# A hybrid decoder layer on one core: the MLP output of seven blocks as seven quarter products of sums

## The chip, the cores and the metric

One NeuronCore of one Trainium2 chip runs the whole layer in one launch. The metric is the device time of that launch in microseconds (us). Engines are named as the profile names them: PE is TensorE, DVE is VectorE, ACT is ScalarE, POOL is GpSimd, SP is SyncE, which here only issues transfers.

## The reference, cut to what matters

The layer works on 512 tokens of 1024 features: a gated linear recurrence and a sparse attention side by side, an output projection, and then the MLP, which is the part that the change touches.

```python
hm = rms_norm(x, mlp_norm_g[l])                                     # 512 x 1024
x = x + jnp.square(jax.nn.relu(hm @ w_mlp_in[l])) @ w_mlp_out[l]    # 1024 x 4096, 4096 x 1024
return rms_norm(x, final_norm_g)
```

## The kernel before

All weights come from HBM as one stream of slabs, 128 partitions x 1024 float32 (512 KB), in the order of use. Slab n goes into `raw[n % 4]`. ScalarE copies it to float32r (`hi`, L553, the high part `whi`), VectorE subtracts that from it (`lo`, L792, the rest, `wlo`), and TensorE multiplies in three passes (`three`, L1154 to L1156): high by high, high by low, low by high. Activations are split in the same way. So every product costs three matmuls, and every slab one ScalarE and one VectorE instruction of 128x1024.

Ahead of the MLP come 55 slabs (`PLAN`) with the mixers as side work. The last of them are those of `w_o`; their results are added to the residual `y` by VectorE (L884). Then TensorE transposes `y`, ScalarE and VectorE split it to `hTh` and `hTl`, and the MLP begins.

The MLP runs over eight blocks of 512 hidden features (`block_` on each engine, seven times in a loop and once more behind it). A block has eight slabs:

- m = 0 to 3, the hidden product: each slab gives 128 hidden features for all 512 tokens, 8 x 3 = 24 matmuls of 512 columns into bank m. ScalarE takes the relu into `rt` (L773), VectorE squares it into `hv` (L1118), ScalarE copies that to float32r `hh` (L775), VectorE subtracts for `hl` (L1121).
- m = 4 to 7, the output product: slab 4 and 5 hold the block's first and second 256 hidden features for output columns 0 to 511, slab 6 and 7 for columns 512 to 1023. Four token tiles x two feature tiles x three passes are 24 matmuls each. Banks 4 to 7 take the first half of the columns, banks 0 to 3 the second. After slab 5 and slab 7 VectorE adds four banks to `y`, scaled by each token's norm factor `r2y` (L1135), eight instructions a block.

Slabs are split three ahead (`AHEAD`) of the one that TensorE works on. Each engine works off its own instructions in the order in which they are written; semaphores count what is done: `raw_in` (slab landed), `hi_done`, `lo_done`, `full[b]` (a bank's sum is complete), `free[b]` (a bank was read out). SP asks for slab n when slab n - 4 has been split (L440). Behind the last block ScalarE sums the squares of `y`, GpSimd forms the norm factor, VectorE scales (L1107), and SP writes `out`.

Of the kernel before, what the change touches and what calls it, by code (L numbers as in the profile page):

```python
# [18 lines left out]
F32 = mybir.dt.float32  # L19
F32R = mybir.dt.float32r  # L20
# [5 lines left out]
P = 128  # L26
T = 512
# [39 lines left out]
V_COLS = 32  # L67
WIN = 2 * P
# [4 lines left out]
def build(nc, x, slabs, vecs, consts, onehot, rel_bias, final_g, out):  # L73
    with ExitStack() as ctx:
# [6 lines left out]
        def sem(name):  # L81
# [61 lines left out]
        hv = [place(f"hv{i}", 189 + 2 * i, T) for i in range(2)]  # L143
# [30 lines left out]
        raw_in = [sem(f"raw_in{s}") for s in range(SLOTS)]  # L174
        hi_done, lo_done, slab_used = sem("hi_done"), sem("lo_done"), sem("slab_used")
# [11 lines left out]
                 "rik_done ry_done rf_done pool_step iqh_done aqh_done kdh_done ikh_done ikl_done")  # L187
# [154 lines left out]
        def used_up(n, it=None):  # L342

            if it is not None:
                m = n - NPLAN
                if m in (4, 6):
                    return slab_used, it * 2 + (BY_COUNT + m // 2 - 1)
                if m == 5:
                    return full[7], it + (MB2[3] + 1)
                if m in (-1, 7):  # L350
                    return full[3], it * 2 + (MB if m == -1 else MB + 2)
                return full[m], it * 2 + (MB + 1)
            if n in by_count:
                return slab_used, by_count[n]
            b, u = c1_bank if tiles[n] == "side" else tiles[n][-1]
            return full[b], u + 1

        def loop_blocks(eng, body):

            with eng.Fori(0, NFB - 1, 1) as it:  # L360
                body(it, False)
            body(NFB - 1, True)
# [32 lines left out]
        mxl3 = mxl[:, :].rearrange("p (k t) -> p k t", k=KD_)  # L395
        hh3 = hh[:, :].rearrange("p (k t) -> p k t", k=4)
# [31 lines left out]
        def _(sp):  # L428
# [5 lines left out]
            def load(n, dyn=None):  # L434

                s = n % SLOTS
                if n >= SLOTS:

                    sp.wait_ge(lo_done, n - SLOTS + 1 if dyn is None else dyn * PER_FB + (n - SLOTS + 1))
                sp.dma_start(raw[s][:, :], slabs[n] if dyn is None else  # L440
                             slabs[bass.ds(dyn * PER_FB + n, 1), :, :].rearrange("a p c -> (a p) c")
                             ).then_inc(raw_in[s], 16)
# [14 lines left out]
            with sp.Fori(0, NFB, 1) as it:  # L457
                for m in range(PER_FB):
                    load(NPLAN + m, it)
# [8 lines left out]
        def _(pool):  # L468
# [61 lines left out]
            for n in range(NPLAN):  # L530
                for s in side[n]:
                    do_side(s)
            pool.wait_ge(S["sq_done"], SQ_Y + NT)
# [11 lines left out]
        def _(act):  # L545
            def hi(n, it=None):

                s = n % SLOTS
                arrived = 16 * (n // SLOTS + 1)
                act.wait_ge(raw_in[s], arrived if it is None else it * (16 * PER_FB // SLOTS) + arrived)  # L550
                if n >= SLOTS:
                    act.wait_ge(*used_up(n - SLOTS, it))
                act.copy(whi[s][:, :], raw[s][:, :]).then_inc(hi_done, 1)  # L553
# [213 lines left out]
            def block_(it, last):  # L767
                for m in range(PER_FB):
                    if not (last and m + AHEAD >= PER_FB):
                        hi(NPLAN + m + AHEAD, it)  # L770
                    if m < 4:
                        act.wait_ge(full[m], it * 2 + (MB + 1))
                        act.activation(rt[m % 2][:, :], bank[m][:, :], ACT.Relu).then_inc(free[m], 1)  # L773
                        act.wait_ge(S["hv_done"], it * 4 + (m + 1))
                        act.activation(hh3[:, m, :], hv[m % 2][:, :], ACT.Copy).then_inc(S["hh_done"], 1)  # L775

            loop_blocks(act, block_)
            for t in range(NT):
                act.wait_ge(free[4 + t], MB2[t] + NFB)
                square(y3[:, t, 0:512], 512, ssf[:, t:t + 1])  # L780
            for t in range(NT):
                act.wait_ge(free[t], MB + 2 * NFB)
                square(y3[:, t, 512:D], 512, ssg[:, t:t + 1])
# [3 lines left out]
        def _(dve):  # L787
            def lo(n, it=None):

                s = n % SLOTS  # L790
                dve.wait_ge(hi_done, n + 1 if it is None else it * PER_FB + (n + 1))
# [318 lines left out]
            def block_(it, last):  # L1110
                for m in range(PER_FB):
                    if not (last and m + AHEAD >= PER_FB):
                        lo(NPLAN + m + AHEAD, it)
                    if m < 4:
                        dve.wait_ge(free[m], it * 2 + (MB + 1))
                        if m:
                            dve.wait_ge(S["hl_done"], it * 4 + m)
                        dve.tensor_tensor(hv[m % 2][:, :], rt[m % 2][:, :], rt[m % 2][:, :],  # L1118
                                          ALU.mult).then_inc(S["hv_done"], 1)
                        dve.wait_ge(S["hh_done"], it * 4 + (m + 1))  # L1120
                        dve.tensor_tensor(hl3[:, m, :], hv[m % 2][:, :], hh3[:, m, :].bitcast(F32),  # L1121
                                          ALU.subtract).then_inc(S["hl_done"], 1)
                    if m in (5, 7):
                        half = (m - 5) // 2
                        if half == 0:
                            dve.wait_ge(S["hl_done"], it * 4 + 4)
                        for t in range(NT):
                            if half == 0:
                                b = 4 + t
                                dve.wait_ge(full[b], it + (MB2[t] + 1))  # L1130
                            else:
                                b = t
                                dve.wait_ge(full[b], it * 2 + (MB + 2))
                            yy = y3[:, t, half * 512:(half + 1) * 512]
                            dve.scalar_tensor_tensor(out=yy, in0=bank[b][:, :], scalar=r2y[:, t:t + 1], in1=yy,  # L1135
                                                     op0=ALU.mult, op1=ALU.add).then_inc(free[b], 1)
                            if last and half == 1 and t:
                                final(t - 1)

            dve.wait_ge(S["ry_done"], 1)  # L1140
            dve.wait_ge(fg_in, 16)
            loop_blocks(dve, block_)
# [4 lines left out]
        def _(pe):  # L1147
# [251 lines left out]
            def block_(it, last):  # L1399
                for m in range(PER_FB):  # L1400
                    n = NPLAN + m
                    s = n % SLOTS
                    pe.wait_ge(lo_done, it * PER_FB + (n + 1))
                    if m < 4:
                        wh, wl = slab_view(whi, s, KD_), slab_view(wlo, s, KD_)
                        pe.wait_ge(free[m], it * 2 + MB)
                        for q, k in enumerate(MLP_K):
                            if m == 0:
                                pe.wait_ge(free[k], mlp_bank[k][1] + 1)
                            ins = three(bank[m][:, :], wh[:, k, :], wl[:, k, :], hTh3[:, k, :], hTl3[:, k, :],  # L1410
                                        q == 0, q == KD_ - 1)
                        ins.then_inc(full[m], 1)
                    else:
                        wh, wl = slab_view(whi, s, 2), slab_view(wlo, s, 2)
                        first, k0 = m % 2 == 0, 2 * (m % 2)
                        for t in range(NT):
                            for kk in range(2):
                                k = k0 + kk
                                if m < 6 and t == 0:
                                    pe.wait_ge(S["hl_done"], it * 4 + (k + 1))  # L1420
                                b = 4 + t if m < 6 else t
                                if first and kk == 0:
                                    pe.wait_ge(free[b], it + MB2[t] if m < 6 else it * 2 + (MB + 1))
                                ins = three(bank[b][:, :], hh3[:, k, t * P:(t + 1) * P], hl3[:, k, t * P:(t + 1) * P],
                                            wh[:, kk, :], wl[:, kk, :], first and kk == 0, k == 3)
                                if k == 3:
                                    ins.then_inc(full[b], 1)
                        if first:
                            ins.then_inc(slab_used, 1)

            loop_blocks(pe, block_)
# [84 lines left out]
```

## Time and profile before

| | |
|---|---|
| device time, median of 3 runs | 795.92 us (795.9 to 798.9) |
| the profiled execution | 796.67 us, its span 794.6 us |
| PE busy | 760.7 us, 96% |
| VectorE busy | 468.0 us, 59% |
| ScalarE busy | 302.2 us, 38% |
| GpSimd busy | 57.3 us, 7% |

The span is the time from the first to the last recorded instruction; the device time has some 2 us around it. Busy time of PE is the union of records that overlap each other, since matmuls are pipelined; the cost of one is read from the distance between the starts of two neighbours. "Idle before" in the grouped rows is the time that the engine stood still in front of such an instruction, and behind the arrow is what ended it.

### The profile page before, as it was taken

What the parts mean: (1) busy time and instruction counts of PE and PEld (TensorE: products, weight loads), DVE (VectorE), ACT (ScalarE), POOL (GpSimd) and SP (SyncE); (2) the same over time, 40 slices, a digit from 0 to 9 for tenths busy, and PEclk for the clock granted to TensorE, in tenths of its full rate; (3) what the DMA queues carried; (4) which work ended last, traced back from release to release, by engine and by line L of the source; (5) the groups of instructions that cost most, each with busy time, mean ns of one, the idle gap of its engine ahead of it and who ended that gap; (6) DMA issues with size and microseconds to landing.
All of it is one profiled execution on the core that took longest, in us unless ns stands there. A gap on an engine that the chain in (4) does not pass through costs nothing.

```text
span 794.6 us, 9959 instructions
## 1 busy us (share of the span) xinstructions
PE 760.7 (96%) x3686; PEld 636.5 (80%) x3686; DVE 468.0 (59%) x756; ACT 302.2 (38%) x495; POOL 57.3 (7%) x94
## 2 busy tenths in 40 slices
PE   5999999899997999999999999999999999999995
PEld 5788888887776788888888888888888888888884
DVE  4567878649999885334834545545445454445444
ACT  6453334547433344433312722323231423232231
POOL 3000010011001144400000000000000000000003
PEclk9999999999997999999999999999999999999998
DMA  7422111212122121112542232333233232323202
GB/s 276 160 80 81 54 54 53 80 54 91 43 85 75 54 80 54 54 59 75 168 178 80 77 109 79 106 100 106 85 97 105 89 106 79 106 89 103 72 1 106
DMA packets 20720, 71.46 MB, mean 90 GB/s; under 512 B 2344, under 2 KB 3536, under 8 KB 20688
## 3 DMA queue, kind: packets, MB, share of 16 engines
q1 hardware_dynamic: 19120, 67.88, 25.7%
q10 hardware_dynamic: 1568, 3.15, 1.1%
q8 instruction: 20, 0.33, 0.2%
q14 instruction: 12, 0.10, 0.0%
HBM read 68.91 MB, written 2.11 MB: 89 GB/s over the span
## 4 chain that ended last, share of the span: by engine, by line
PE 83%; DVE 11%; issue 2%; ACT 2%; DMA 0%; POOL 0%; DVEq 0%; POOLq 0%; ACTq 0%; SPq 0%
PE bank L1154 24%; PE bank L1156 24%; PE bank L1155 24%; PE bank L1283 3%; PE bank L1371 2%; DVE sc L948 2%; DVE small L945 2%; PE bank L1162 1%; DVE wlo L792 1%; DVE sc L935 1%; PE bank L1169 1%; PE bank L1355 1%; DVE aqs L842 1%; PE bank L1356 1%; DVE hO L1049 1%
## 5 line engine op out<-in xcount | busy, mean ns | idle before, releaser
L792 DVE TENSOR_TENSOR wlo<-raw,whi 128x1024 fp32r<-128x1024 f32 x119 | 146.2, 1229 | 112.2 <-ACT whi L553 106.7
L1154 PE MATMUL bank<-hTh,whi 128*128 128x512 f32 (+1 forms) x456 | 181.0, 397 | 3.1 <-DVE aqs L842 1.9
L1156 PE MATMUL bank<-hTh,wlo 128*128 128x512 f32 (+1 forms) x456 | 178.7, 392 | 0.0
L1155 PE MATMUL bank<-hTl,whi 128*128 128x512 f32 (+1 forms) x456 | 178.5, 391 | 0.0
L553 ACT CAST whi<-raw 128x1024 fp32r<-128x1024 f32 x119 | 124.2, 1044 | 139.3 <-PE bank L1156 139.1
L1154 PEld LDWEIGHTS bank<-hTh,whi 128*128 128x128 f32 (+1 forms) x456 | 86.0, 189 | 23.1 <-issue 4.4
L1156 PEld LDWEIGHTS bank<-hTh,wlo 128*128 128x128 f32 (+1 forms) x456 | 85.8, 188 | 18.7
L1155 PEld LDWEIGHTS bank<-hTl,whi 128*128 128x128 f32 (+1 forms) x456 | 86.0, 188 | 18.4 <-issue 0.5
L1154 PE MATMUL bank<-whi,hh 128*128 128x512 f32 x256 | 99.6, 389 | 0.0
L1155 PE MATMUL bank<-wlo,hh 128*128 128x512 f32 x256 | 99.6, 389 | 0.0
L1156 PE MATMUL bank<-whi,hl 128*128 128x512 f32 x256 | 99.6, 389 | 0.0
L1118 DVE TENSOR_TENSOR hv<-rt 128x512 f32<-128x512 f32 x32 | 22.1, 692 | 67.6 <-ACT rt L773 67.6
L1135 DVE SCALAR_TENSOR_TENSOR y<-bank,small,y 128x512 f32<-128x512 f32 x64 | 46.7, 747 | 25.9 <-PE bank L1156 25.9
L1155 PEld LDWEIGHTS bank<-wlo,hh 128*128 128x128 f32 x256 | 48.1, 188 | 10.0
L1154 PEld LDWEIGHTS bank<-whi,hh 128*128 128x128 f32 x256 | 48.1, 188 | 9.9
L1156 PEld LDWEIGHTS bank<-whi,hl 128*128 128x128 f32 x256 | 48.1, 188 | 9.9
L773 ACT ACTIVATE rt<-bank 128x512 f32<-128x512 f32 x32 | 19.1, 597 | 86.4 <-PE bank L1156 86.4
L1154 PE MATMUL bank<-whi,hTh 128*128 128x512 f32 x96 | 38.1, 397 | 2.0 <-DVE iqs L842 2.0
L1156 PE MATMUL bank<-whi,hTl 128*128 128x512 f32 x96 | 37.5, 391 | 0.0
L1155 PE MATMUL bank<-wlo,hTh 128*128 128x512 f32 x96 | 37.4, 390 | 0.0
L729 ACT ACTIVATE et<-bank 128x128 f32<-128x128 f32 (+3 forms) x32 | 14.0, 436 | 60.0 <-PE bank L1162 59.7
L1121 DVE TENSOR_TENSOR hl<-hv,hh 128x512 fp32r<-128x512 f32 x32 | 22.2, 693 | 22.4 <-ACT hh L775 22.4
(182 smaller groups left out, 1030.8 us busy)
## 6 DMA issues: line engine op xcount, KB each, us to landing
raw<-slabs SPq DMA_DIRECT2D x119, 512.0 KB, 3.3
xs<-x SPq DMA_DIRECT2D x4, 512.0 KB, 4.9
y<-x ACTq DMA_DIRECT2D x1, 2048.0 KB, 8.9
out<-ys SPq DMA_DIRECT2D x3, 512.0 KB, 2.6
bt<-bias_rows ACTq DMA_DIRECT2D x1, 1024.0 KB, 5.2
cst<-consts SPq DMA_DIRECT2D x1, 608.0 KB, 9.6
fg<-final_g SPq DMA_DIRECT2D x1, 512.0 KB, 7.3
out<-ys SPq DMA_DIRECT2D x2, 256.0 KB, 2.1
```

Source lines behind the costliest of these rows:

```text
L553: act.copy(whi[s][:, :], raw[s][:, :]).then_inc(hi_done, 1)
L773: act.activation(rt[m % 2][:, :], bank[m][:, :], ACT.Relu).then_inc(free[m], 1)
L792: dve.tensor_tensor(wlo[s][:, :], raw[s][:, :], whi[s][:, :].bitcast(F32), ALU.subtract).then_inc(lo_done, 1)
L945: dve.max(mx8[:, 8 * (i - 1):8 * i], sc_of(i)).then_inc(S["max_done"], 1)
L948: dve.match_replace(sc_of(i), mx8[:, 8 * (i - 1):8 * i], sc_of(i), TAKEN).then_inc(S["rep_done"], 1)
L1118: dve.tensor_tensor(hv[m % 2][:, :], rt[m % 2][:, :], rt[m % 2][:, :], ALU.mult).then_inc(S["hv_done"], 1)
L1121: dve.tensor_tensor(hl3[:, m, :], hv[m % 2][:, :], hh3[:, m, :].bitcast(F32), ALU.subtract).then_inc(S["hl_done"], 1)
L1135: dve.scalar_tensor_tensor(out=yy, in0=bank[b][:, :], scalar=r2y[:, t:t + 1], in1=yy, op0=ALU.mult, op1=ALU.add).then_inc(free[b], 1)
L1154: pe.matmul(dst, lh, rh, start=start, stop=False)
L1155: pe.matmul(dst, lh, rl, start=False, stop=False)
L1156: return pe.matmul(dst, ll, rh, start=False, stop=stop)
L1283: ins = pe.matmul(bank[bu[0]][:, 64 * v:64 * v + 64].rearrange("p (n h) -> p n h", h=H), un, rhs, start=True, stop=True)
```

## The change

In the first seven blocks the output product is cut into quarters. The block's squared activations A (512 tokens x 512 features) are four quarters A00, A01, A10, A11 of 256 x 256 (first index: half of the tokens, second: half of the features), the weights B (512 features x 1024 columns) four slabs B11, B12, B21, B22. Instead of eight quarter products there are seven of sums, in this order (`PRODUCTS` names them 1, 7, 4, 5, 6, 3, 2):

| order | left side | right side | banks |
|---|---|---|---|
| 1 | A00 | B11 | 0, 1 |
| 2 | A00 - A10 (`sa`) | B22 - B12 (in `br12`) | 4, 5, kept over all blocks |
| 3 | A11 | `wt4` = `wt2` - B21 | 2, 3 |
| 4 | A10 + A11 (`sb`) | `wt1` = B12 - B11 | 0, 1 |
| 5 | `sb` - A00 (`sx`) | `wt2` = B22 - `wt1` | 2, 3 |
| 6 | A01 - `sx` (`sa` again) | B22 | 0, 1 |
| 7 | A01 | B21 | 6, 7, kept over all blocks |

Each is 2 token tiles x 2 feature tiles x 3 passes = 12 matmuls of 512 columns. VectorE forms the four weight sums (`w_sum`) and the four activation sums (`s_sum`), each left and right side is split in two as before (`a_hi` and `hi_out` on ScalarE, `a_lo` and `lo_out` on VectorE), and products 1, 3, 4, 5 and 6 are added by VectorE from their banks to float32 tiles `acc` (`gather`), two instructions each. The square moves to ScalarE (from `rt` into `hv`, now the whole block). `y` is not touched in these blocks. GpSimd fills the five `acc` tiles with zeros ahead of the MLP and does nothing within it. The four output slabs of a block are loaded to tiles of their own (`br`), which come free in the order of the waits in `load_out`. The eighth block is computed as before; in its hidden product VectorE mixes the seven kept sums to the four quarters of the output and adds them to `y`.

```diff
@@ what may be ahead of what @@
+        NST = NFB - 1
+        WPB = 4 + len(PRODUCTS)
+        PBANKS = ((0, 1), (4, 5), (2, 3), (0, 1), (2, 3), (0, 1), (6, 7))
+        KEPT = (1, 6)
+        USE_B = [4, 4, 3, 3]
@@ SP @@
+            def load_out(it):
+                for k, m, after in (("11", 4, WPB - 3), ("12", 6, WPB - 5), ("22", 7, WPB - 1), ("21", 5, WPB)):
+                    sp.wait_ge(lo_done, it * WPB + (NPLAN - WPB + after))
+                    sp.dma_start(br[k][:, :], mlp_slab(m, it)).then_inc(br_in[k], 16)
...
+            sp.wait_ge(full[b], u + 1)
+            with sp.Fori(0, NST, 1) as it:
+                load_out(it)
+                for m in range(4):
+                    sp.wait_ge(lo_done, it * WPB + (NPLAN + m + 1))
+                    sp.dma_start(raw[(NPLAN + m) % SLOTS][:, :], mlp_slab(m, it + 1)
@@ POOL @@
+            for p in acc:
+                pool.memset(acc[p][:, :], 0.0).then_inc(S["acc_zero"], 1)
@@ ACT @@
+            def relu(m, it):
+                act.wait_ge(full[m], in_use(m, it) + 1)
+                act.activation(rt[m % 2][:, :], bank[m][:, :], ACT.Relu).then_inc(free[m], 1)
+                act.wait_ge(free[m], in_use(m, it) + 1)
+                act.activation(hv3[:, m, :], rt[m % 2][:, :], ACT.Square).then_inc(S["hv_done"], 1)
...
+                relu(3, it)
+                hi_out(3, it)
+                a_hi(2, it, "hv_done", 4)
+                a_hi(3, it, "s_done", 2)
+                act.wait_ge(*product_full(0, 1, it))
+                hi_out(4, it)
+                a_hi(4, it, "s_done", 3)
+                act.wait_ge(*product_full(1, 1, it))
+                hi_out(5, it)
+                a_hi(5, it, "s_done", 4)
+                act.wait_ge(*product_full(2, 1, it))
+                hi_out(6, it)
+                a_hi(6, it, "hv_done", 4)
+                act.wait_ge(*product_full(4, 1, it))
+                hi_in(0, it + 1)
...
@@ DVE @@
+            def gather(p, it):
+                for q in range(2):
+                    b = PBANKS[p][q]
+                    dve.wait_ge(*product_full(p, q, it))
+                    a_ = acc[PRODUCTS[p]][:, q * T:(q + 1) * T]
+                    dve.tensor_tensor(a_, bank[b][:, :], a_, ALU.add).then_inc(free[b], 1)
+            def block_(it):
+                lo_in(3, it)
...
+                w_sum(wt1, br["12"], br["11"], 0, it)
+                lo_out(0, it)
...
+                w_sum(br["12"], br["22"], br["12"], 1, it)
+                s_sum(sa, a_part(0, 0), a_part(1, 0), ALU.subtract, it, 2)
+                a_lo(0, it)
+                lo_out(1, it)
+                w_sum(wt2, br["22"], wt1, 2, it)
...
+                w_sum(wt4, wt2, br["21"], 3, it)
+                a_lo(1, it)
+                lo_out(2, it)
+                s_sum(sb, a_part(1, 0), a_part(1, 1), ALU.add, it, 4)
+                s_sum(sx, two(sb), a_part(0, 0), ALU.subtract, it, 0, 2)
+                a_lo(2, it)
+                lo_out(3, it)
+                a_lo(3, it)
+                gather(0, it)
+                dve.wait_ge(S["al_done"], it * 7 + 2)
+                s_sum(sa, a_part(0, 1), two(sx), ALU.subtract, it, 0, 3)
+                a_lo(4, it)
+                lo_out(4, it)
+                lo_out(5, it)
+                a_lo(5, it)
+                gather(2, it)
+                a_lo(6, it)
+                lo_out(6, it)
+                gather(3, it)
+                gather(4, it)
+                lo_in(0, it + 1)
+                gather(5, it)
+                lo_in(1, it + 1)
+                lo_in(2, it + 1)
@@ PE @@
+                for p in range(len(PRODUCTS)):
...
+                    pe.wait_ge(lo_done, it * WPB + (NPLAN + 4 + p + 1))
+                    pe.wait_ge(S["al_done"], it * 7 + (p + 1))
+                    for q in range(2):
+                        b = PBANKS[p][q]
+                        if not kept:
+                            pe.wait_ge(free[b], out_use(p, q, it))
...
+                        for kk in range(2):
+                            ins = three(bank[b][:, :], two(ah[p])[:, kk, q * P:(q + 1) * P],
+                                        two(al[p])[:, kk, q * P:(q + 1) * P], wh[:, kk, :], wl[:, kk, :],
```

In the code products, operands and gathers are counted from 0 (`gather(2)` is that of the third product).

## Rows read from the trace of the kernel before

**Rows 1.** The page, busy time by engine, and the chain by engine.
```profile
PE 760.7 (96%) x3686; PEld 636.5 (80%) x3686; DVE 468.0 (59%) x756; ACT 302.2 (38%) x495; POOL 57.3 (7%) x94
PE 83%; DVE 11%; issue 2%; ACT 2%; DMA 0%; POOL 0%; DVEq 0%; POOLq 0%; ACTq 0%; SPq 0%
```
**Rows 2.** Windows, the MLP: from:to length, busy (instructions), granted clock, DMA share, GB/s.
```profile
437.00:785.00 348.00, 348.00 (x1536) 288.01 (x1534) 167.55 (x194) 110.88 (x149) 3.33 (x7) 1.00 0.26 86
```
**Rows 3.** Timeline of PE: start, length, what.
```profile
436.68 0.50 PE L1154 MATMUL bank<-hTh,whi 128*128 128x512 f32 x1 [0.48 <-DVE hTl L812]
437.01 0.39 PE L1155 MATMUL bank<-hTl,whi 128*128 128x512 f32 x1
...
480.34 0.39 PE L1154 MATMUL bank<-hTh,whi 128*128 128x512 f32 x1
...
784.75 0.39 PE L1156 MATMUL bank<-whi,hl 128*128 128x512 f32 x1
```
**Rows 4.** Grouped instructions, 440 to 790 us: busy, mean ns | idle before.
```profile
L792 DVE TENSOR_TENSOR wlo<-raw,whi 128x1024 fp32r<-128x1024 f32 x61 | 74.7, 1225 | 63.9 <-ACT whi L553 58.6 <-POOL small L536 5.3
L553 ACT CAST whi<-raw 128x1024 fp32r<-128x1024 f32 x61 | 63.8, 1046 | 109.7 <-PE bank L1156 109.7
...
L1135 DVE SCALAR_TENSOR_TENSOR y<-bank,small,y 128x512 f32<-128x512 f32 x64 | 46.7, 747 | 25.9 <-PE bank L1156 25.9
...
L1118 DVE TENSOR_TENSOR hv<-rt 128x512 f32<-128x512 f32 x32 | 22.1, 692 | 67.6 <-ACT rt L773 67.6
L775 ACT ACTIVATE hh<-hv 128x512 fp32r<-128x512 f32 x32 | 20.3, 633 | 26.5 <-DVE hv L1118 26.5
L773 ACT ACTIVATE rt<-bank 128x512 f32<-128x512 f32 x32 | 19.1, 597 | 86.4 <-PE bank L1156 86.4
L565 ACT ACTIVATE junk<-y 128x512 f32<-128x512 f32 x8 | 5.1, 631 | 16.7 <-DVE y L1135 16.7
```
**Rows 5.** Timeline of DVE, neighbours that don't depend on each other.
```profile
476.18 1.23 DVE L792 TENSOR_TENSOR wlo<-raw,whi 128x1024 fp32r<-128x1024 f32 x1 [4.21 <-ACT whi L553]
477.33 1.40 DVE L1135 SCALAR_TENSOR_TENSOR y<-bank,small,y 128x512 f32<-128x512 f32 x2
...
361.32 2.48 DVE L1083 TENSOR_TENSOR obl<-bank,obh 128x512 fp32r<-128x512 f32 x4 [5.20 <-ACT obh L583]
```
**Rows 6.** Timeline of DVE, the second waits for the first.
```profile
255.51 0.55 DVE L948 MATCH_REPLACE8 sc<-small,sc 128x384 f32<-128x384 f32 x1
256.09 0.56 DVE L945 MAX8 small<-sc 128x8 f32<-128x384 f32 x1
```
**Rows 7.** Timelines of ACT and DVE, a relu and the square behind it.
```profile
485.98 0.60 ACT L773 ACTIVATE rt<-bank 128x512 f32<-128x512 f32 x1 [4.38 <-PE bank L1156]
...
486.61 0.69 DVE L1118 TENSOR_TENSOR hv<-rt 128x512 f32<-128x512 f32 x1 [3.76 <-ACT rt L773]
```
**Rows 8.** Timeline of ACT, the second waits for the first.
```profile
440.02 0.25 ACT L565 ACTIVATION_READ_ACCUMULATOR junk<-y 128x1 f32 x1
440.36 1.06 ACT L565 ACTIVATE junk<-y 128x1024 f32<-128x1024 f32 x1
```
**Rows 9.** The chain in order of time, in front of the first MLP matmul.
```profile
435.21 1.42 DVE hTl L812 x2
```
**Rows 10.** Windows, and timeline of PE: waits of TensorE and the granted clock.
```profile
240.00:250.00 10.00, 6.72 (x19) 5.40 (x20) 9.10 (x25) 2.96 (x9) 1.32 (x3) 0.53 0.15 52
...
260.00:300.00 40.00, 37.37 (x201) 31.23 (x200) 35.10 (x98) 16.95 (x45) 12.28 (x18) 1.00 0.21 67
...
243.28 0.48 PE L1355 MATMUL bank<-kdh,aqs 128*128 128x128 f32 x1 [4.59 <-DVE small L1066]
...
279.10 0.63 PE L1371 MATMUL bank<-c0s,et 128*128 128x64 f32 x4 [1.06 <-DVE ob L1077]
```
**Rows 11.** The page, loads of slabs; grouped instructions, a zero fill.
```profile
raw<-slabs SPq DMA_DIRECT2D x119, 512.0 KB, 3.3
...
L483 POOL MEMSET hA<- 128x2048 f32 x1 | 1.8, 1804 | 0.1
```

More of the change, by code:

```diff
@@ L340, in build, with used_up @@
         BY_COUNT = seen
[L342 to L352, printed above, removed]
+        def used_up(n):
             if n in by_count:
@@ L765, in _ @@
                 square(y3[:, t, :], D, ssy[:, t:t + 1])
[L767 to L775, printed above, removed]
@@ new lines, in last_ @@
+            def last_(it):
+                for m in range(4):
+                    if m == 0:
+                        hi_in(3, it)
+                    else:
+                        act.wait_ge(full[m - 1], in_use(m - 1, it) + 1)
+                        k = m - 1
+                        act.wait_ge(br_in[w_last_in[k]], it * 16 + 16)
+                        s = (NPLAN + 4 + k) % SLOTS
+                        act.copy(whi[s][:, :], w_last[k][:, :]).then_inc(hi_done, 1)
+                    relu(m, it)
+                    act.wait_ge(S["hv_done"], it * 4 + (m + 1))
+                    act.activation(hh3[:, m, :], hv3[:, m, :], ACT.Copy).then_inc(S["hh_done"], 1)
+                act.wait_ge(br_in[w_last_in[3]], it * 16 + 16)
+                s = (NPLAN + 7) % SLOTS
+                act.copy(whi[s][:, :], w_last[3][:, :]).then_inc(hi_done, 1)
@@ L1108, in final @@
                                              op0=ALU.mult, op1=ALU.mult).then_inc(S["fin_done"], 1)
[L1110 to L1124, printed above, removed]
-                        if half == 0:
[L1126 to L1138, printed above, removed]
@@ L1140, in _, with lo_op, lo_in, lo_out @@
-            dve.wait_ge(S["ry_done"], 1)
+            def lo_op(q, src, it):
+                s = (NPLAN + q) % SLOTS
+                dve.wait_ge(hi_done, it * WPB + (NPLAN + q + 1))
+                dve.tensor_tensor(wlo[s][:, :], src[:, :], whi[s][:, :].bitcast(F32), ALU.subtract).then_inc(lo_done, 1)
+            def lo_in(m, it):
+                lo_op(m, raw[(NPLAN + m) % SLOTS], it)
+            def lo_out(k, it):
+                lo_op(4 + k, w_src[k], it)
+            def w_sum(out_, a_, b_, after, it):
+                if after:
+                    dve.wait_ge(S["wt_done"], it * 4 + after)
+                dve.tensor_tensor(out_[:, :], a_[:, :], b_[:, :], ALU.subtract).then_inc(S["wt_done"], 1)
@@ L1141, in _ @@
             dve.wait_ge(fg_in, 16)
-            loop_blocks(dve, block_)
+            dve.wait_ge(S["acc_zero"], len(acc))
+            loop_blocks(dve, block_, last_)
             final(NT - 1)
@@ L1397, in _ @@
                 transposes(mlp_bank[k], [y3[:, t, k * P:(k + 1) * P] for t in range(NT)])
[L1399 to L1429, printed above, removed]
@@ L1431, in _, with hidden @@
-            loop_blocks(pe, block_)
+            def hidden(m, it):
+                s = (NPLAN + m) % SLOTS
+                wh, wl = slab_view(whi, s, KD_), slab_view(wlo, s, KD_)
+                pe.wait_ge(lo_done, it * WPB + (NPLAN + m + 1))
+                pe.wait_ge(free[m], in_use(m, it))
+                for q, k in enumerate(MLP_K):
+                    if m == 0:
+                        pe.wait_ge(free[k], mlp_bank[k][1] + 1)
+                    ins = three(bank[m][:, :], wh[:, k, :], wl[:, k, :], hTh3[:, k, :], hTl3[:, k, :],
+                                q == 0, q == KD_ - 1)
+                ins.then_inc(full[m], 1)
@@ new lines, in block_ @@
+            def block_(it, begin=False, end=False):
+                for m in range(4):
+                    hidden(m, it)
+                for p in range(len(PRODUCTS)):
+                    s = (NPLAN + 4 + p) % SLOTS
+                    wh, wl = slab_view(whi, s, 2), slab_view(wlo, s, 2)
+                    kept = p in KEPT
+                    pe.wait_ge(lo_done, it * WPB + (NPLAN + 4 + p + 1))
+                    pe.wait_ge(S["al_done"], it * 7 + (p + 1))
+                    for q in range(2):
+                        b = PBANKS[p][q]
+                        if not kept:
+                            pe.wait_ge(free[b], out_use(p, q, it))
+                        elif begin:
+                            pe.wait_ge(free[b], MB2[b - 4])
+                        for kk in range(2):
+                            ins = three(bank[b][:, :], two(ah[p])[:, kk, q * P:(q + 1) * P],
+                                        two(al[p])[:, kk, q * P:(q + 1) * P], wh[:, kk, :], wl[:, kk, :],
+                                        (begin or not kept) and kk == 0, (end or not kept) and kk == 1)
+                        ins.then_inc(full[b], 1)
@@ new lines, in last_ @@
+            def last_(it):
+                for m in range(4):
+                    hidden(m, it)
+                for m in range(4, PER_FB):
+                    s = (NPLAN + m) % SLOTS
+                    wh, wl = slab_view(whi, s, 2), slab_view(wlo, s, 2)
+                    first, k0 = m % 2 == 0, 2 * (m % 2)
+                    pe.wait_ge(lo_done, it * WPB + (NPLAN + m + 1))
+                    for t in range(NT):
+                        b = 4 + t if m < 6 else t
+                        for kk in range(2):
+                            k = k0 + kk
+                            if m < 6 and t == 0:
+                                pe.wait_ge(S["hl_done"], k + 1)
+                            if first and kk == 0:
+                                pe.wait_ge(free[b], MB2[t] + 1 if m < 6 else in_use(t, it) + 1)
+                            ins = three(bank[b][:, :], hh3[:, k, t * P:(t + 1) * P], hl3[:, k, t * P:(t + 1) * P],
+                                        wh[:, kk, :], wl[:, kk, :], first and kk == 0, k == 3)
+                            if k == 3:
+                                ins.then_inc(full[b], 1)
@@ L1435, in constants @@
+            block_(0, begin=True)
+            with pe.Fori(1, NST - 1, 1) as it:
+                block_(it)
+            block_(NST - 1, end=True)
+            last_(NST)
 def constants():
```

177 lines of the change are left out of this document (154 added, 23 removed).

## The prediction

> **What bounds the kernel now.** I read the page's busy shares first, then the chain, then the MLP stretch by windows, then TensorE's timeline there, then the grouped instructions and single lines of VectorE's and ScalarE's timelines. The page gives TensorE 96% of the span, VectorE 59%, ScalarE 38%, and the chain that ended last is 83% TensorE [rows 1]. In the stretch from 437 to 785 us, the whole MLP, TensorE is busy for 348.00 of 348.00 us at a granted clock of 1.00, while VectorE works 167.6 and ScalarE 110.9 us [rows 2]. The matmuls of it start at 437.01 and 784.75 with 1534 steps between them, so one costs (784.75 - 437.01) / 1534 = 0.2267 us; a record's 0.39 us is its latency and not its price [rows 3]. A block of 192 matmuls is 43.52 us (the second block starts at 480.34, 192 steps after 436.68 plus the slow first step) [rows 3]. So the MLP is bound by TensorE's count of matmuls, and by nothing else: removing matmuls gains time until another engine can no longer keep ahead.
>
> **What the change removes.** A block's output product was 4 slabs x 4 token tiles x 2 feature tiles x 3 passes = 96 matmuls. In seven blocks it becomes 7 products x 2 token tiles x 2 feature tiles x 3 passes = 84, of the same shape (128x128 against 512 columns). The hidden product keeps its 96, the eighth block keeps 192. Removed are 7 x 12 = 84 matmuls, 84 x 0.2267 = 19.04 us, if TensorE never waits. A changed block is then 180 x 0.2267 = 40.80 us.
>
> **What it adds, by engine and per changed block.** VectorE had 8 weight remainders at 1.225, 8 multiplies and subtractions of 0.69 and 8 updates of y at 0.747: 21.3 us. It gets 11 remainders and 4 weight sums of the same 128x1024 form (15 x 1.225 = 18.4) and 4 activation sums, 7 remainders and 10 gathers of 128x512 (21 x 0.69 = 14.5): 32.9 us of 40.8. ScalarE had 8 x 1.046 + 4 x 0.597 + 4 x 0.633 = 13.3 us and gets 11 x 1.046 + 4 x 0.597 + 4 x 0.631 (the squares, priced by the 128x512 square of the end) + 7 x 0.633 = 20.9 us [rows 4]. Both fit; ScalarE loosely. VectorE at 81% is not hidden by that sum: what counts is its order, because 20 of its instructions can only run after the last hidden tile is out.
>
> **Prices for the walk.** A following VectorE instruction starts before the record of the one in front ends: 477.33 - 476.18 = 1.15 us behind a 128x1024 one, and four 128x512 subtractions with a PSUM bank as input take 2.48, that is 0.69 + 3 x 0.60 [rows 5]; by the same 0.09 of overlap I take 1.23 - 0.09 = 1.14 behind the wide ones. These four have the gather's form (bank and SBUF in, SBUF out), so a gather is 0.60 to the next. Behind its own result an instruction starts 0.03 after the end [rows 6]; I use 0.02 to 0.03. A result goes from ScalarE to VectorE in 486.61 - (485.98 + 0.60) = 0.03 [rows 7], taken as 0.04. The relu starts 0.20 after the slot in which its last matmul ends: 480.34 + 24 x 0.2267 = 485.78 against 485.98 [rows 3, 7]. ScalarE behind its own result starts 0.09 later (440.27 to 440.36) [rows 8]. When TensorE waited for VectorE it began 0.05 after (435.21 + 1.42 = 436.63 to 436.68), and its first step took 0.33 and not 0.23 [rows 3, 9]: a release costs 0.15 in all.
>
> The Trainium skill (VectorE: DVE Perf Modes, the section on the TRN2 errata) prices an instruction from PSUM 62 cycles above one from SBUF, at 0.96 GHz 0.065 us. By an estimate from that page the five gathers in the chain below would take 0.3 us more per block, 2.3 us in all. The trace differs: the four with a bank as input keep 0.60 to the next, and L1118, all SBUF, has the same 0.69 [rows 4, 5]; the rows decide.
>
> **The walk through a changed block**, in us from the start of its first matmul; the products are numbered 1 to 7 in the order in which TensorE does them. Hidden tiles end at 5.44, 10.88, 16.32, 21.76. Until then VectorE is ahead: the split of the three last hidden slabs, the weight sums, and the first two products' operands are done by about 20.4 (the remainder of the second product's left side, which waits behind relu 2 on ScalarE), and these products are due at 21.76 and 24.48. After the last tile: relu 21.96 to 22.56, square 22.65 to 23.28. VectorE: sum b 23.31, sum x 24.02, then the third left remainder, which waits for ScalarE's copy (queued behind the weight copy, 23.19 + 0.94, + 0.63 = 24.76): 24.80. Then one after the other: weight remainder 25.40, left remainder 26.54, gather of product 1 at 27.14 and 27.74, sum a 28.34, left remainder 28.94, two weight remainders 29.54 and 30.68, left remainder 31.82, gather of product 3 at 32.42 (out 33.11) and 33.02, left remainder 33.62, weight remainder 34.22, gather of product 4 at 35.36, out 36.05.
> TensorE: products 1 to 4 are due at 21.76, 24.48, 27.20 and 29.92 and find everything there (the closest: left remainder 4 out at 27.2, and bank 0 free at 27.8, for 29.92). Product 5 writes bank 2, so it waits for the gather of product 3: due 32.64, released 33.11, effective start 33.26, a stall of 0.62. It ends at 35.98. Product 6 needs bank 0, so the gather of product 4: 36.05 + 0.15 = 36.20, a stall of 0.22. Product 7 has its operands at 35.4 and is due at 38.92. The block ends at 41.64. The first three slabs of the next block are split behind products 5, 6 and 7 (the first at 38.9, due 41.64), so no stall there. **0.84 us of stall per block.**
>
> **The other edits.** Each block still loads 8 slabs of 512 KB, which land in 3.3 us [rows 11]; the four output slabs are asked for at 26.5 to 35.5 of the block before and needed from 4.8 on, some 10 us of cover. SP's queue holds the hidden slabs behind the output slabs, and they are needed some 35 us later: nothing. In the first block the output slabs wait for the last matmul of w_o, the transposes of y come between, and the first two are needed 3.7 us into the block, so over 5 us after they are asked for: nothing; if one landed 5 us late it would cost at most that once. VectorE no longer waits for the row statistics before the first block, but TensorE had no idle time there: no gain. The five zero fills on GpSimd: 0.9 us each by half of the 128x2048 one (1.80) [rows 11], when GpSimd is idle and VectorE's mixing runs some 5 us ahead of its use: nothing. The last block adds on VectorE five 128x1024 mixes, two additions from PSUM and eight updates of y, 6.1 + 1.4 + 6.0 us, over the hidden product's 21.8 us together with its 4 splits: done by about 20; the banks that the output products need come free at 15 at the latest. The tail behind the last matmul is the same code: 9.6 us as before.
>
> **Sum.** 7 x (43.52 - 41.64) = 13.2 us. The profiled execution took 796.67 (span 794.6), so 783.5; the median of the runs shown is 795.92, 0.75 below it, so **782.7 us**. Both ends of the unknown: below, no stall at all (the chain 0.84 shorter), 19.04 us: 776.9. Above, no overlap between neighbouring VectorE instructions.
>
> **Rivals.**
> (a) TensorE never stalls: 776.9. It needs VectorE's chain from the last tile to the fourth gather to take 13.4 instead of 14.3 us. Against it: every duration has a row and the order is in the code. For it: a few records overlap more than I allow.
> (b) VectorE's chain doesn't overlap, since nearly every instruction in it now carries a wait. With 0.09 more on each of 13 steps from 25.40 to 35.36, 1.17 per block, the block takes 42.81: 7 x 0.71 = 5.0 us gained, 790.9. For it: the chain has more waits than any stretch of before. Against it: the y updates carry a wait each and still start 1.15 behind a weight remainder [rows 5].
> (c) Slower than before: the stalls bring TensorE's clock down. In the trace a wait of 4.59 us was followed by matmuls at half clock: 240 to 250 us shows 0.53, and as TensorE came back at 243.28 about 6 us were run at 1.2 GHz instead of 2.4, 3.0 us lost [rows 10]. Once per block that is 7 x 3.0 = 21 us: 803.7; it turns the sign from 13.2 / 3.0 = 4.4 blocks on. Against it: between 260 and 300 us there was a wait of 1.06 us and the clock stayed at 1.00 [rows 10], and mine are 0.6 and 0.2.
> The Trainium skill (TensorE: Matmul & The Clock Gate, "A second HAM failure mode") says that short frequent pauses between groups of matmuls that cycle through PSUM banks can let the clock swing between its two levels; that is (c)'s rule. The trace of before bears it out only behind the long wait.
> (d) The chain's balance is wrong in another way: a wait that I placed early is late (the second product's operands, the first slab's split), beyond the 2.72 us per block that one product is worth. Then the kernel is slower too, by 1 us per block or so: about 803.
>
> **Chances.** Forecast (781 to 786) 0.68; (a) 0.09; (b) and halfway to it 0.15; (c) 0.04; (d) 0.04. The range goes from (a) to (b): 777 to 791. A difference under 0.5%, 4.0 us, could not be told from none. Faster by more than that, below 791.9: 0.86 (all of the forecast and (a), most of (b)); same 0.08; slower 0.06.
>
> **What the new profile would show.** 84 matmuls fewer (3602 in all). In each changed block TensorE idle for about 0.4 us in front of product 5, released by VectorE's gather into acc (a record shows 0.16 us less than the stall in starts), and a trace of it in front of product 6; a block step of 41.6 us. VectorE busy about 557 us (468 + 7 x 11.6 + 8), ScalarE about 355 (302 + 7 x 7.6). Clock 1.00 throughout. If the idle stands in front of products 2 or 3, or is released by whi, wlo or al, the walk is wrong; if the step is 40.8, (a); near 42.8 with spaced VectorE records, (b). I would be wrong altogether if the interval between matmuls changed within groups of six per bank.

## The result, and the profile after

The changed kernel takes 783.79 us (median of 4 runs, 783.18 to 785.04) against 795.94 us of the kernel before beside it; the ratio is 0.984, with a 95% interval of 0.982 to 0.986. Forecast were 782.7 us, range 777 to 791. Two executions of this study enter no ratio, the profiled one of the first experiment at 1721.11 us and one of the kernel before at 1288.17 us; the others of these two kernels took 782 to 799 us.

The page of the changed kernel, busy time by engine and the chain by engine, answers to [rows 1]; below it the windows view from 450 to 760 us, all within the seven changed blocks.

```profile
PE 748.1 (96%) x3602; PEld 621.7 (79%) x3602; DVE 544.9 (70%) x853; ACT 353.2 (45%) x569; POOL 62.6 (8%) x99
PE 72%; DVE 16%; issue 5%; ACT 4%; POOL 1%; DMA 1%; DVEq 0%; POOLq 0%; ACTq 0%; SPq 0%
```
```profile
450.00:760.00 310.00, 307.82 (x1344) 250.88 (x1343) 233.14 (x277) 147.73 (x196) 0.00 (x0) 1.00 0.27 89
```

84 matmuls are gone (3686 to 3602), the clock in the blocks is 1.00, and TensorE now has 2 us without work in 310, where it had none [rows 2].

TensorE's timeline of the second changed block, against [rows 3]: the block's first matmul, the first of the fifth product, the first of the sixth with the one in front of it, the next block's first, and the last of the MLP.

```profile
480.42 0.39 PE L1390 MATMUL bank<-hTh,whi 128*128 128x512 f32 x1
...
513.50 0.50 PE L1390 MATMUL bank<-whi,ah 128*128 128x512 f32 x1 [0.28 <-DVE acc L1270]
...
516.12 0.39 PE L1392 MATMUL bank<-whi,al 128*128 128x512 f32 x1
516.43 0.50 PE L1390 MATMUL bank<-whi,ah 128*128 128x512 f32 x1
...
522.00 0.39 PE L1390 MATMUL bank<-hTh,whi 128*128 128x512 f32 x1
...
773.39 0.39 PE L1392 MATMUL bank<-whi,hl 128*128 128x512 f32 x1
```

The fifth product starts 33.08 us into the block (walked: 33.16), the sixth 36.01 us (walked: 36.10, of which 0.05 is the restart), and the step is 41.58; the six steps from here on are 41.58 to 41.65. Walked were 41.64. In front of the sixth product no idle time is written, yet the starts are 0.31 apart and not 0.23: a stall shorter than a record's overhang doesn't show as idle, only in the starts.

VectorE's timeline, the end of its chain in that block:

```profile
511.02 1.22 DVE L1237 TENSOR_TENSOR wlo<-br,whi 128x1024 fp32r<-128x1024 f32 x1
512.16 0.69 DVE L1262 TENSOR_TENSOR al<-sa,ah 128x512 fp32r<-128x512 f32 x1
512.76 1.28 DVE L1270 TENSOR_TENSOR acc<-bank,acc 128x512 f32<-128x512 f32 x2
513.96 0.68 DVE L1262 TENSOR_TENSOR al<-hv,ah 128x512 fp32r<-128x512 f32 x1
514.56 1.22 DVE L1237 TENSOR_TENSOR wlo<-br,whi 128x1024 fp32r<-128x1024 f32 x1
515.69 1.88 DVE L1270 TENSOR_TENSOR acc<-bank,acc 128x512 f32<-128x512 f32 x3
```

No row has idle time in front. The first gather of the third product starts at 512.76, 32.34 into the block, and frees bank 2 some 0.69 later, 0.05 before TensorE's restart; the first of the fourth starts at 35.27. The distances are 1.13 to 1.14 and 0.60 throughout, as priced from [rows 5].

Two of the grouped rows of the MLP stretch: the gather, and the square on ScalarE.

```profile
L1270 DVE TENSOR_TENSOR acc<-bank,acc 128x512 f32<-128x512 f32 x70 | 44.3, 682 | 0.0
...
L835 ACT ACTIVATE hv<-rt 128x512 f32<-128x512 f32 x32 | 20.3, 633 | 1.0
```

The MLP as a whole, from first to last matmul start, went from 784.75 - 436.68 = 348.07 us [rows 3] to 773.39 - 438.62 = 334.77: 13.30 us less, forecast 13.2.

### The profile page after: what moved, and what is told of

The parts are those of the page before. It is cut to its first block, busy times and chain, and to the rows that moved or that the text cites. A ratio compares the mean times of both kernels' runs of the same rounds, so it can differ in the third digit from the quotient of the medians.

```text
span 783.2 us, 10090 instructions
## 1 busy us (share of the span) xinstructions
PE 748.1 (96%) x3602; PEld 621.7 (79%) x3602; DVE 544.9 (70%) x853; ACT 353.2 (45%) x569; POOL 62.6 (8%) x99
## 4 chain that ended last, share of the span: by engine, by line
PE 72%; DVE 16%; issue 5%; ACT 4%; POOL 1%; DMA 1%; DVEq 0%; POOLq 0%; ACTq 0%; SPq 0%
PE bank L1390 21%; PE bank L1392 20%; PE bank L1391 20%; PE bank L1519 3%; DVE sc L1071 2%; PE bank L1607 2%; DVE small L1068 2%; DVE acc L1270 2%; PE bank L1398 1%; DVE wlo L915 1%; DVE wlo L1237 1%; DVE al L1262 1%; DVE sc L1058 1%; ACT whi L829 1%; PE bank L1405 1%
## 5 line engine op out<-in xcount | busy, mean ns | idle before, releaser
L915 DVE TENSOR_TENSOR wlo<-raw,whi 128x1024 fp32r<-128x1024 f32 x58 | 71.2, 1229 | 48.3 <-ACT whi L606 48.2
L1390 PE MATMUL bank<-whi,ah 128*128 128x512 f32 x196 | 77.8, 397 | 2.2 <-DVE acc L1270 2.2
L1391 PE MATMUL bank<-wlo,ah 128*128 128x512 f32 x196 | 76.4, 390 | 0.0
L1392 PE MATMUL bank<-whi,al 128*128 128x512 f32 x196 | 76.4, 390 | 0.0
L606 ACT CAST whi<-raw 128x1024 fp32r<-128x1024 f32 x58 | 60.5, 1044 | 29.6 <-PE bank L1392 29.3
L824 ACT CAST whi<-raw 128x1024 fp32r<-128x1024 f32 x29 | 29.8, 1052 | 56.1 <-PE bank L1392 56.1
L1237 DVE TENSOR_TENSOR wlo<-br,whi 128x1024 fp32r<-128x1024 f32 x32 | 39.1, 1221 | 18.8 <-ACT whi L829 18.5
L1390 PEld LDWEIGHTS bank<-whi,ah 128*128 128x128 f32 x196 | 36.8, 188 | 14.6 <-DVE acc L1270 5.2
L1237 DVE TENSOR_TENSOR wlo<-raw,whi 128x1024 fp32r<-128x1024 f32 x29 | 34.8, 1222 | 15.6 <-ACT whi L824 15.1
L1270 DVE TENSOR_TENSOR acc<-bank,acc 128x512 f32<-128x512 f32 x70 | 44.3, 682 | 0.0
L1392 PEld LDWEIGHTS bank<-whi,al 128*128 128x128 f32 x196 | 36.8, 188 | 7.9
L1391 PEld LDWEIGHTS bank<-wlo,ah 128*128 128x128 f32 x196 | 36.8, 188 | 7.2
```

Of the source, the lines that this page charges most:

```text
L915: dve.tensor_tensor(wlo[s][:, :], raw[s][:, :], whi[s][:, :].bitcast(F32), ALU.subtract).then_inc(lo_done, 1)
L1237: dve.tensor_tensor(wlo[s][:, :], src[:, :], whi[s][:, :].bitcast(F32), ALU.subtract).then_inc(lo_done, 1)
L1270: dve.tensor_tensor(a_, bank[b][:, :], a_, ALU.add).then_inc(free[b], 1)
L1390: pe.matmul(dst, lh, rh, start=start, stop=False)
L1391: pe.matmul(dst, lh, rl, start=False, stop=False)
L1392: return pe.matmul(dst, ll, rh, start=False, stop=stop)
```

## The experiments

### The gather of the third product alone moved up

```diff
                 lo_out(4, it)
+                gather(2, it)
                 lo_out(5, it)
                 a_lo(5, it)
-                gather(2, it)
                 a_lo(6, it)
```


> The changed kernel, with VectorE's gather of the third product moved up by two instructions, ahead of the sixth product's weight and left remainders (1.14 + 0.60 us earlier). Theory (the whole chain of VectorE from the last hidden tile to the gather of the fourth product sets the block): the wait in front of the fifth product goes, and all of it, 0.6 to 0.8 us, comes back in front of the sixth; block step 41.6 us as before it, time 783.8 us. Rival (the wait in front of the fifth product is itself what costs): 7 x 0.62 = 4.3 us gained, 779.5 us.

Measured: 781.84, 781.88, 783.45 and 785.75 us, ratio to the kernel before 0.982 (0.979 to 0.985). For the block step the same kernel ran again:

> The gather of the third product alone moved up, once more, for its block step, which a disturbed profile did not give. Theory (the chain to the gather of the fourth product sets the block): step 41.6 us, the wait now 0.6 to 0.8 us in front of the sixth product. Rival (the wait on bank 2 is itself what costs): step 41.0 us.

783.05 us, 0.982 (0.980 to 0.984). TensorE's timeline: two block starts and the one row between them with idle time.

```profile
478.08 0.39 PE L1390 MATMUL bank<-hTh,whi 128*128 128x512 f32 x1
...
514.09 0.50 PE L1390 MATMUL bank<-whi,ah 128*128 128x512 f32 x1 [0.49 <-DVE acc L1270]
...
519.66 0.39 PE L1390 MATMUL bank<-hTh,whi 128*128 128x512 f32 x1
```

The wait now stands 36.01 us into the block, which is the sixth product, and the step is 41.58 as before. Taking away the first wait moved the loss and gained nothing: what sets the block is the whole of VectorE's chain up to the gather of the fourth product.

### Both gathers moved up

```diff
                 lo_out(4, it)
+                gather(2, it)
                 lo_out(5, it)
                 a_lo(5, it)
-                gather(2, it)
+                gather(3, it)
                 a_lo(6, it)
                 lo_out(6, it)
-                gather(3, it)
                 gather(4, it)
```


> The changed kernel, with the gather of the third product moved up as in the run before, and the gather of the fourth moved up by two instructions as well, ahead of the seventh product's left and weight remainders. Theory: VectorE then frees bank 2 at 31.3 us and bank 0 at 34.3 us into the block, before TensorE wants them (32.6 and 35.4); the seventh product's operands are out at 36.6, wanted at 38.1; no stall is left, block step 40.8 us, 7 x 0.82 = 5.7 us less: 778.1 us. Rival (VectorE is simply too loaded, a later wait takes its place): step stays at 41.6, 783.8 us, with the wait in front of the seventh product or the next block's first tile.

778.18 us median of 5 runs (776.03 to 779.62), ratio 0.9755 (0.973 to 0.978): faster than both kernels.

```profile
476.27 0.39 PE L1390 MATMUL bank<-hTh,whi 128*128 128x512 f32 x1
...
517.07 0.39 PE L1390 MATMUL bank<-hTh,whi 128*128 128x512 f32 x1
```
```profile
450.00:760.00 310.00, 310.00 (x1369) 256.72 (x1368) 232.45 (x277) 147.59 (x199) 0.00 (x0) 1.00 0.26 88
```

The step is 40.80, which is 180 x 0.2267, and from 450 to 760 us TensorE is busy for 310.00 of 310.00. VectorE does the same work as in the changed kernel, 232.45 us in this window against 233.14; only the order of it differs. So the stall was a matter of what VectorE did first: it had prepared operands of the seventh product, due last, ahead of freeing a bank that was due sooner.

### The fourth product done twice

```diff
-                        for kk in range(2):
+                        for kk in (0, 1, 0, 1) if p == 3 else (0, 1):
```


> The changed kernel, with the fourth product's 12 matmuls done twice in each of the seven blocks (the second time overwrites the first), so that TensorE has its 192 matmuls per block back, with all else of the change in place. Theory (the gain is the count of matmuls, less the stalls): the 2.72 us swallow the stall, block step 43.52 us, 783.8 + 7 x 1.90 = 797.1 us, as before the change within 0.3%. Rival (the change also gains by taking the y updates off VectorE, or loses by its other work): away from 796 by more than 2 us.

796.87 us median of 10 runs, ratio to the kernel before 0.9992 (0.998 to 1.001). Block step 525.13 - 481.61 = 43.52:

```profile
481.61 0.39 PE L1390 MATMUL bank<-hTh,whi 128*128 128x512 f32 x1
...
525.13 0.39 PE L1390 MATMUL bank<-hTh,whi 128*128 128x512 f32 x1
```

With TensorE's twelve matmuls given back, the whole gain is gone, and not more than it: by the interval, all else of the change together (sums, gathers, squares, the y updates that are gone, the loads in another order) is worth at most 1.7 us either way. That holds while TensorE has 192 matmuls per block to cover VectorE's chain, as the step without a stall shows; with 180 the same chain costs the 0.8 us of a block.

### The squares back on VectorE

```diff
 ScalarE, for each hidden tile
-                relu(m, it)
+                act.wait_ge(full[m], in_use(m, it) + 1)
+                if m >= 2:
+                    act.wait_ge(S["hv_done"], it * 4 + (m - 1))
+                act.activation(rt[m % 2][:, :], bank[m][:, :], ACT.Relu).then_inc(free[m], 1)
 VectorE, ahead of the instruction that needs it (before `s_sum(sb, ...)` for the last tile)
+                dve.wait_ge(free[m], in_use(m, it) + 1)
+                dve.tensor_tensor(hv3[:, m, :], rt[m % 2][:, :], rt[m % 2][:, :], ALU.mult).then_inc(S["hv_done"], 1)
```


> The changed kernel, with the four squares of each of the seven blocks back on VectorE (right in front of the instruction that needs them). Theory (only the chain behind the last hidden tile counts, and there a square costs the same on either engine, 0.69 + 0.04 against 0.63 + 0.09, while ScalarE's copies come 0.6 us sooner): block step 41.4 to 41.6 us, 782.5 to 783.8 us, though VectorE is busy for 35.7 of 41.6 us. Rival (VectorE's load counts: 4 x 0.60 = 2.4 us more per block): 783.8 + 16.8 = 800.6 us.

782.73 us, ratio 0.982 (0.980 to 0.984). The page and two block starts:

```profile
PE 746.3 (96%) x3602; PEld 620.1 (79%) x3602; DVE 562.8 (72%) x881; ACT 336.5 (43%) x541; POOL 61.5 (8%) x99
```
```profile
478.00 0.39 PE L1404 MATMUL bank<-hTh,whi 128*128 128x512 f32 x1
...
519.55 0.39 PE L1404 MATMUL bank<-hTh,whi 128*128 128x512 f32 x1
```

VectorE works 18 us longer, and the step is 0.03 to 0.11 us shorter (the six are 41.51 to 41.60), as the chain says. The part of the change that relieves VectorE of the squares bought nothing: three of the four stand where VectorE waits anyway (in that block it still idles 1.49 us in front of the first, 2.14 in front of the second and 1.04 behind the third), and behind the fourth the third left remainder starts 24.65 us into the block, against 24.72 in the changed kernel.

### One more VectorE instruction, in either order

```diff
                 s_sum(sa, a_part(0, 1), two(sx), ALU.subtract, it, 0, 3)
+                dve.tensor_tensor(pad[:, :], fg[:, 0:T], fg[:, T:D], ALU.subtract).then_inc(S["pad_done"], 1)
```
The lines that declare the tile `pad` and the semaphore `pad_done` are left out here. In the changed kernel:

> The changed kernel, with one more 128x512 subtraction on VectorE in each of the seven blocks, behind the sum for the sixth product's left side (its result is not used). Theory: VectorE's chain behind the last hidden tile has no slack, so its 0.60 us shows in full: block step 42.2 us, 783.8 + 4.2 = 788.0 us. Rival (VectorE idles for 8 us of a block, which hides it): no change, 783.8.

In the kernel with both gathers early:

> The kernel with both gathers early, with the same one more 128x512 subtraction on VectorE at the same place. Theory: there bank 2 comes free at 31.9 us and bank 0 at 34.9 us, wanted at 32.6 and 35.4, so it is hidden: block step 40.8 us, 778.2 us. Rival (VectorE's work costs wherever it stands): 7 x 0.60 = 4.2 us more, 782.4 us.

Measured: 788.35 us (ratio 0.989, 0.987 to 0.991) and 778.14 us (0.976, 0.974 to 0.979). Block starts in the first, then in the second:

```profile
479.53 0.39 PE L1395 MATMUL bank<-hTh,whi 128*128 128x512 f32 x1
...
513.22 0.50 PE L1395 MATMUL bank<-whi,ah 128*128 128x512 f32 x1 [0.89 <-DVE acc L1271]
...
521.76 0.39 PE L1395 MATMUL bank<-hTh,whi 128*128 128x512 f32 x1
```
```profile
478.02 0.39 PE L1395 MATMUL bank<-hTh,whi 128*128 128x512 f32 x1
...
518.82 0.39 PE L1395 MATMUL bank<-hTh,whi 128*128 128x512 f32 x1
```

Steps 42.23 and 40.80. The same instruction at the same place costs its full 0.60 us per block in one order and nothing in the other, with VectorE idle for some 11 us of the block in the first (31.14 busy of 42.23) and 10 in the second (31.05 of 40.80).

### Longer waits and the clock

Three and seven such instructions, each behind the one before, in the changed kernel:

```diff
+                for i in range(3):          # and range(7)
+                    if i:
+                        dve.wait_ge(S["pad_done"], it * 3 + i)
+                    dve.tensor_tensor(pad[:, :], fg[:, 0:T], fg[:, T:D], ALU.subtract).then_inc(S["pad_done"], 1)
```
Seven:

> The changed kernel, with seven more 128x512 subtractions on VectorE at the same place, each waiting for the one before (6 x 0.71 + 0.60 = 4.86 us in all), so that TensorE stands still for over 5 us once per block. If waits cost only themselves: block step 46.5 us, 783.8 + 34.0 = 817.8 us, clock 1.00. If such a wait brings the clock down as the one of 4.6 us ahead of the MLP does, some 6 us at half clock behind each: 3 us more per block, step 49.5, 838.8 us. For the change itself: only if already the clock of the stretches behind its waits of 0.6 us fell would that rival be alive.

Three:

> The changed kernel with three more 128x512 subtractions on VectorE at the same place (2 x 0.71 + 0.60 = 2.02 us), so that TensorE stands still for some 2.3 us once per block. If waits cost only themselves: block step 43.6 us, 783.8 + 14.1 = 797.9 us. If waits of this length already bring the clock down, as those of 5.3 us did at 1.6 us per block: step 45.2 us, 809 us. Ahead of the MLP a wait of 1.99 us left the clock alone in one profile and brought it down in another, so some blocks of the seven may show it and others not.

Seven: 827.54 us, ratio 1.038 (1.036 to 1.041). Three: 803.07 us, 1.006 (1.004 to 1.008). Windows of the one with seven, around the wait of 5.2 us that ends at 522.71:

```profile
520.00:524.00 4.00, 1.29 (x3) 1.10 (x4) 4.00 (x7) 0.00 (x0) 0.00 (x0) 0.50 0.35 103
524.00:526.00 2.00, 2.00 (x6) 1.51 (x6) 2.00 (x3) 0.00 (x0) 0.00 (x0) 0.50 0.14 55
526.00:528.00 2.00, 2.00 (x9) 1.58 (x8) 1.11 (x3) 0.24 (x1) 0.00 (x0) 0.79 0.77 262
528.00:530.00 2.00, 2.00 (x11) 1.64 (x10) 1.52 (x3) 0.82 (x1) 0.00 (x0) 1.00 0.00 0
```

The granted clock is 0.50, that is 1.2 of 2.4 GHz, for over 4 us behind the wait, and it had fallen before the wait ended, since all of 520 to 524 us shows 0.50. The seven steps average (772.44 - 435.77) / 7 = 48.1 us where waits alone would give 46.5: 1.6 us a block for the clock, from 2.4 in the first block (step 48.90) to 1.3 in the last (47.84). Neither of the two forecasts for this run, 817.8 and 838.8 us, was met; the measured time lies between them. With three, TensorE's timeline and windows, one block that fell and the next that did not:

```profile
606.28 0.80 PE L1395 MATMUL bank<-whi,ah 128*128 128x512 f32 x1 [2.33 <-DVE acc L1271]
...
651.26 0.50 PE L1395 MATMUL bank<-whi,ah 128*128 128x512 f32 x1 [2.33 <-DVE acc L1271]
```
```profile
568.00:612.00 44.00, 41.67 (x177) 34.12 (x176) 31.88 (x39) 19.72 (x26) 0.00 (x0) 0.96 0.29 95
612.00:656.00 44.00, 41.67 (x183) 33.92 (x183) 32.67 (x40) 19.78 (x27) 0.00 (x0) 1.00 0.27 94
```

The same wait of 2.33 us, the same code: behind the first the matmul record is 0.80 us long and the block's mean clock 0.96, behind the second 0.50 and 1.00. The steps are 45.23, 44.91, 43.68, 44.98, 43.63, 45.02, 43.70: four blocks with the clock down, three at the 43.6 that waits alone give, 1.3 us apart.

## Why the prediction was right

- **The removed matmuls.** 84 x 0.2267 us was exact: with the stall gone the step is 40.80, with the matmuls back it is 43.52.
- **The stall.** 0.84 us a block forecast, (19.04 - 13.30) / 7 = 0.82 measured. In the block shown it is 0.78, of it 0.54 in front of the fifth product and 0.24 in front of the sixth; walked were 0.62 and 0.22. It came out because the walk priced each instruction by the distance to the next (1.14, 0.60) and not by its record (1.23, 0.69); by the records the chain would have been rival (b), 790.9 us, which the VectorE rows above refute. It lay where it was put: moving one gather moved it, moving both removed it. So rival (a), a step of 40.80, and rival (b), one of 42.81, are out; and so is (d), because in the changed blocks every row of TensorE with idle time in front is released by a gather (L1270), none by an operand.
- **PSUM as a source.** The changed trace has 0.682 us for the gather from a bank and 0.69 for the remainders from SBUF. Both are 0.60 to the next. The surcharge of the Trainium skill (VectorE: DVE Perf Modes, the section on the TRN2 errata) is not there for this form; 2.3 us by that estimate would have been too many.
- **Edits costed at nothing.** Loads, zero fills, the tail (9.8 us behind the last matmul start in both traces) and the eighth block (43.29 us from its first matmul start to its last in both) showed nothing. The doubled product bounds all of them together: 0.9992 (0.998 to 1.001) of the time before.
- **The clock, rival (c).** A real mechanism, and too far away to decide here: in the changed blocks waits of 0.2 to 1.0 us left the clock at 1.00, those of 2.33 us brought it down in four blocks of seven, those of 5.2 us in all. Its price was too high in the forecast, 3.0 us against 1.3 to 1.6 on average. Most of the difference is the length of the half clock: 6.0 us behind the wait at 243.28 in the kernel before, from which the price was taken, 4.1 us in the block shown above of the kernel with seven and some 3.3 us behind the wait that ends at 606.28 in the kernel with three. A further 0.2 us is not lost, since VectorE goes on meanwhile and the wait in front of the sixth product vanishes. The rule of the Trainium skill (TensorE: Matmul & The Clock Gate, "A second HAM failure mode"), that short frequent pauses between groups make the clock swing, did not show in the changed blocks, where such a pause comes once or twice in 42 us. Ahead of the MLP the changed kernel's trace does show a fall of this kind: behind a stretch of short matmuls at 253 to 256 us whose longest wait is 0.67 us, the clock stood at 0.50. Three of the ten profiles read here have it (longest wait 0.65 to 0.73 us), the others do not, three of them with a wait of 0.85 to 0.92 us there. TensorE's timeline and windows of the changed kernel:

```profile
254.55 0.41 PE L1607 MATMUL bank<-c0s,et 128*128 128x64 f32 x2 [0.67 <-DVE ob L1200]
```
```profile
254.00:256.00 2.00, 1.34 (x8) 1.17 (x9) 1.31 (x10) 1.77 (x9) 1.31 (x3) 0.96 0.62 197
256.00:258.00 2.00, 2.00 (x6) 1.56 (x5) 1.90 (x7) 1.47 (x3) 0.06 (x1) 0.50 0.19 74
```

So the trace agrees with the page there and not in the changed blocks, and that a short wait leaves the clock alone is shown for these blocks only.
- **What was mis-sized.** VectorE's busy time was forecast at 557 us and is 544.9: I summed records, while busy time counts the 0.09 us by which neighbours overlap only once. ScalarE, which has few close neighbours, came to 353.2 against 355. VectorE's instructions in the queue from sum b to the gather of the sixth product are 22, not 20. None of these numbers enters the time.
- **The last microsecond.** The median is 1.1 us above the forecast and the profiled execution 1.5 us (785.04 against 783.5), though the MLP gained 13.3 us. In the profiled execution the MLP began 1.94 us later, in code that the change doesn't touch. 0.3 us of it is there from the beginning. 1.6 us arise behind a wait of 1.99 us, which both kernels have at 148.6 to 148.9 us and which is shown here. The same happens behind a wait of 1.92 us at 200.16 (1.93 at 198.26 in the kernel before, clock 1.00), another 1.6 us. Of this lag of 3.5 us, 1.9 are gone by 244.86, where TensorE comes back from a wait for VectorE of 4.46 us (4.59, up to 243.28, before); the half clock behind that wait costs 0.35 us less than before, and the fall at 256 us 0.7 more. Windows of the kernel before, then of the changed kernel:

```profile
150.00:152.00 2.00, 2.00 (x10) 1.67 (x9) 1.91 (x5) 0.93 (x1) 0.00 (x0) 1.00 0.00 0
152.00:154.00 2.00, 2.00 (x10) 1.65 (x10) 1.15 (x1) 0.00 (x0) 0.00 (x0) 1.00 0.00 0
```
```profile
150.00:152.00 2.00, 2.00 (x7) 1.52 (x6) 1.94 (x4) 1.23 (x2) 0.00 (x0) 0.50 0.00 0
152.00:154.00 2.00, 2.00 (x8) 1.59 (x7) 1.42 (x2) 0.00 (x0) 0.00 (x0) 0.64 0.00 0
```

Over the profiles of this study the MLP begins anywhere from 435.34 to 438.62 us, and beside the experiments the kernel before had medians of 797.5 to 797.6 and not 795.9. So single microseconds of the whole time are the luck of the clock ahead of the MLP, and that the forecast met the median to 1.1 us is in part such luck: from 797.5 the same gain leads to 784.2. The block step repeats to a few hundredths.

## What to carry to other kernels

Fewer matmuls by sums of operands paid their exact count here, as long as the chain of the helper engine (VectorE) behind the last input it must wait for is shorter than the products that cover it; walk that chain with start-to-start distances, and don't look at the engine's busy share. On the helper's queue, free the accumulator bank that is wanted next before preparing operands that are wanted last: that order alone was worth 5.6 us (783.79 to 778.18). And when one wait is removed, ask what the same queue makes late next, since a wait that only moves gains nothing.

## What was not expected of the hardware

A wait of TensorE of 1.9 to 2.4 us is a coin toss for its clock. In the same program it fell in four of seven blocks behind waits of 2.33 to 2.43 us. Ahead of the MLP, in ten profiles, it fell five times behind the wait of 1.98 to 2.00 us at 148 us and eight times behind that of 1.90 to 1.94 us at 198 to 200 us, so the longer wait is not the surer one; what decides it no run here shows. Each fall behind 2.33 us costs 1.3 us. A kernel with waits of that length has a spread of its own, and the waits cost more than their length: three extra VectorE instructions, 2.0 us a block, made the kernel 0.6% (0.4 to 0.8) slower than the one before the change, 803.07 us where waits alone would have given 797.9; the difference is the price of the four falls in its profile (4 x 1.3 = 5.2 us).
